# First feed-forward: unnormalized token halves, the inverse root applied to the gate and up products, context transposes within the projection

## What is computed

```python
def rms_norm(x, w):
    y = x * rsqrt(mean(x * x, -1) + EPS)
    return y * w
...
        mixed = concatenate([fox_out, hgrn_out], -1) @ w_out[l]
        h = h + mixed
        u = rms_norm(h, norm_ffn_w[l])
        h = h + (silu(u @ w_ffn_gate[l]) * (u @ w_ffn_up[l])) @ w_ffn_down[l]
```

## Time and profile before

| | us |
|---|---|
| median of 3 runs | 2755.51 |
| lowest, highest | 2754.37, 2759.36 |
| the profiled execution | 2757.04 |
| its span on the core | 2755.1 |

### The profile page before, as it was taken

How to read it: one execution, slowest core, us unless ns; L and a number is a source line. 1 busy time by engine, 2 the same in 40 slices (tenths; PEclk the granted TensorE clock), 3 DMA queues, 4 the chain that set the end, 5 groups by cost and what they waited for, 6 DMA issues and landing times.

```text
span 2755.1 us, 36972 instructions
## 1 busy us (share of the span) xinstructions
PE 2569.0 (93%) x14795; PEld 2198.5 (80%) x14795; DVE 1531.8 (56%) x2878; ACT 1096.7 (40%) x1928; POOL 321.7 (12%) x199
## 2 busy tenths in 40 slices
PE   7988889999997999998899999999899998999998
PEld 6787777878886877776788888888788787777877
DVE  3565547657747777677745443436455556533334
ACT  5544534222234655555521211114566556422222
POOL 2222100000012222121000000002223222000001
PEclk9999999999998999999899999999999999999999
DMA  4111033535521111111233333330323222222231
GB/s 118 47 39 51 19 107 122 176 124 181 169 84 47 39 39 39 31 39 39 69 100 123 104 110 113 103 123 24 73 52 73 52 53 60 73 96 86 96 108 47
DMA packets 247333, 223.86 MB, mean 81 GB/s; under 512 B 36916, under 2 KB 215898, under 8 KB 247162
## 3 DMA queue, kind: packets, MB, share of 16 engines
q1 hardware_dynamic: 247162, 221.49, 26.8%
HBM read 219.24 MB, written 2.22 MB: 80 GB/s over the span
## 4 chain that ended last, share of the span: by engine, by line
PE 77%; DVE 11%; ACT 7%; issue 4%; POOL 0%; DMA 0%; SPq 0%; DVEq 0%; POOLq 0%; ACTq 0%
PE ps L363 24%; PE ps L365 22%; PE ps L364 22%; DVE FR L527 2%; ACT FR L522 1%; PE ps L2815 1%; ACT whi L388 1%; PE ps L652 1%; PE ps L1071 1%; PE ps L2401 1%; ACT FA L2494 1%; PE ps L2826 1%; DVE hT L2574 1%; DVE FA L2614 1%; DVE raw L1444 1%
## 5 line engine op out<-in xcount | busy, mean ns | idle before, releaser
L363 PE MATMUL ps<-Uh,whi 128*128 128x512 f32 (+2 forms) x2544 | 904.2, 355 | 25.2 <-ACT FA L2513 5.9
L364 PE MATMUL ps<-Ul,whi 128*128 128x512 f32 (+2 forms) x2544 | 888.3, 349 | 0.0
L365 PE MATMUL ps<-Uh,wlo 128*128 128x512 f32 (+2 forms) x2544 | 887.8, 349 | 0.0
L363 PEld LDWEIGHTS ps<-Uh,whi 128*128 128x128 f32 x2544 | 491.2, 193 | 97.1 <-issue 20.0
L365 PEld LDWEIGHTS ps<-Uh,wlo 128*128 128x128 f32 x2544 | 489.7, 193 | 60.4
L364 PEld LDWEIGHTS ps<-Ul,whi 128*128 128x128 f32 x2544 | 491.2, 193 | 57.7
L388 ACT ACTIVATE whi<-raw 128x1024 fp32r<-128x1024 f32 (+2 forms) x205 | 296.4, 1446 | 555.0 <-PE ps L365 554.8
L399 DVE TENSOR_TENSOR wlo<-raw,whi 128x2048 fp32r<-128x2048 f32 (+2 forms) x121 | 248.3, 2053 | 299.3 <-ACT whi L388 299.1
L363 PE MATMUL ps<-FR,whi 128*128 128x512 f32 (+1 forms) x864 | 305.6, 354 | 24.9 <-DVE FR L527 20.1
L364 PE MATMUL ps<-FR,whi 128*128 128x512 f32 (+1 forms) x864 | 302.2, 350 | 0.0
L365 PE MATMUL ps<-FR,wlo 128*128 128x512 f32 (+1 forms) x864 | 301.8, 349 | 0.0
(11 more groups left out here) (334 smaller groups left out, 3289.0 us busy)
## 6 DMA issues: line engine op xcount, KB each, us to landing
FA<-in_ada_w_dram SPq DMA_DIRECT2D x192, 256.0 KB, 2.8
raw<-in_ffn_w_gate_up_dram SPq DMA_DIRECT2D x44, 1024.0 KB, 5.1
raw<-in_ffn_w_down_dram SPq DMA_DIRECT2D x24, 768.0 KB, 4.3
raw<-in_w_in_dram SPq DMA_DIRECT2D x29, 512.0 KB, 3.9
raw<-in_da_wqkv_dram SPq DMA_DIRECT2D x24, 512.0 KB, 3.7
raw<-in_na_wqkv_dram SPq DMA_DIRECT2D x24, 512.0 KB, 3.8
raw<-in_w_ffn_gate_dram SPq DMA_DIRECT2D x11, 1024.0 KB, 5.3
raw<-in_w_ffn_up_dram SPq DMA_DIRECT2D x11, 1024.0 KB, 5.4
```

Of the source, the lines that this page charges most:

```text
L363: e.matmul(out, ah, bh, start=start, stop=False)
L364: e.matmul(out, ah, bl, start=False, stop=False)
L365: return e.matmul(out, al, bh, start=False, stop=stop)
```

## The change

The high half of block n is made by ACT straight from `hT` with the weight column as scale, and the low half by DVE, both right behind the residual add of the block (`mixed_scalar`, `mixed_vector`). They lack the inverse root. The root is made as before, now into `st_acc`, while PE runs the first gate chunk: the ones matmul stands behind the first gate tile and uses bank 3. The first gate chunk goes tile by tile rather than through both tiles at once. In the feed-forward DVE multiplies each gate product by the root (`v_mul`, out of PSUM into `sil`), ACT takes silu there in place, and DVE multiplies by the root once more (`u_mul`), which stands for the root of the up product. `f_mul` then works as before. All sixteen transposes of the context stand behind block 5 of the projection, two blocks to a bank, and ACT's eight copies ahead of its work on block 6.

```diff
@@ norm_tensor, root_scalar: the bank is given as b; the root goes to st_acc
-        r = K.st_rs[:, t0:t1]
+        r = K.st_acc[:, t0:t1]
...
@@ norm_scalar and norm_vector are gone
@@ def mixed_tensor(K, e, w):
-    context_tensor(K, e, w, range(0, 4))
-    norm_tensor(K, e, w, "f0", (SX,))
-    context_tensor(K, e, w, range(4, 8))
+        if n2 == 2:
+            context_tensor(K, e, w)
@@ def mixed_scalar(K, e, w):
+        if n == 6:
+            for c in range(KC):
+                context_scalar(K, e, w, c)
         w.wait_ge(*K.at("o_add", n))
+        e.activation(K.Uh[:, n, 0:512], K.hT[:, n, 0:512], ACT.Identity, bias=K.zero[:, :], scale=K.cp(col("norm_ffn_w", n))).then_inc(
+            *K.ev("norm_hi", "f0", n, 0))
         square_scalar(K, e, w, "f0", n, 0, *SX)
-    root_scalar(K, e, w, "f0", (SX,))
-    for c in range(KC):
-        w.wait_ge(*K.at("norm_scaled", "f0", c, 0))
-        e.activation(K.Uh[:, c, 0:512], K.st_tmp[:, c % 2, 0:512], ACT.Identity, bias=K.zero[:, :]).then_inc(*K.ev("norm_hi", "f0", c, 0))
-        context_scalar(K, e, w, (0, 7, 1, 2, 3, 4, 5, 6)[c])
-        if c == 3:
-            split_hi(K, e, w)
+    split_hi(K, e, w)
+    root_scalar(K, e, w, "f0", (SX,), 3)
@@ def mixed_vector(K, e, w):
         e.tensor_tensor(hv, K.bank(n), hv, ALU.add).then_inc(*K.ev("o_add", n))
+        w.wait_ge(*K.at("norm_hi", "f0", n, 0))
+        halve_vector(K, e, hv, K.Uh[:, n, 0:512], K.Ul[:, n, 0:512], ("norm_lo", "f0", n, 0), K.cp(col("norm_ffn_w", n)))
         square_vector(K, e, w, "f0", n, 0, *SX)
-    norm_vector(K, e, w, "f0", (SX,), (SX,), lambda c, i: K.cp(col("norm_ffn_w", c)), lambda c, i: K.zero[:, :])
@@ def ffn_tensor(K, e, w, f):
-                o = K.hold(w, b, ("f_silu", st, m + n))[:, 0:t1 - t0]
+                o = K.hold(w, b, ("v_mul" if st == "f0" else "f_silu", st, m + n))[:, 0:t1 - t0]
...
-                project_first(K, e, w, st, len(f.segs), wh, wl, first)
+                for n, (j, i, t0, t1) in enumerate(f.tiles):
+                    t = project_piece(K, e, w, st, 0, first[n][0], wh, wl, t0, t1, j * P)
+                    t.then_inc(*K.ev("f_gate", st, n))
+                    if n == 0:
+                        norm_tensor(K, e, w, "f0", (SX,), 3)
@@ def ffn_scalar(K, e, w, f):
+            if st == "f0":
+                for n in (m, m + 1) if x == 0 else ():
+                    w.wait_ge(*K.at("v_mul", st, n))
+                    e.activation(K.sil[:, n % 2, :], K.sil[:, n % 2, :], ACT.Silu).then_inc(*K.ev("f_silu", st, n))
...
@@ def ffn_vector(K, e, w, f):
+            if x == 0 and st == "f0":
+                w.wait_ge(*K.at("norm_root", st, 0))
+                for n in (m, m + 1):
+                    w.wait_ge(*K.at("f_gate", st, n))
+                    w.wait_ge(*K.was("f_mul", st, n - 2))
+                    e.tensor_tensor(K.sil[:, n % 2, :], K.bank(K.xbank[st, n]), K.st_acc[:, 0:512], ALU.mult).then_inc(
+                        *K.ev("v_mul", st, n))
             if x == 0:
                 split_lo(K, e, w, "wlo_dve")
+            if x == 0 and st == "f0":
+                for n in (m, m + 1):
+                    w.wait_ge(*K.at("f_silu", st, n))
+                    e.tensor_tensor(K.sil[:, n % 2, :], K.sil[:, n % 2, :], K.st_acc[:, 0:512], ALU.mult).then_inc(
+                        *K.ev("u_mul", st, n))
```

More of the change, by code:

```diff
@@ L428, in square_vector, with norm_tensor, root_scalar @@
     e.tensor_tensor(acc, acc, K.st_sq[:, k, 0:t1 - t0], ALU.add).then_inc(*K.ev("square_sum", st, c, i))
-def norm_tensor(K, e, w, st, segs):
+def norm_tensor(K, e, w, st, segs, b):
     for i, (t0, t1) in enumerate(segs):
-        o = K.hold(w, i, ("norm_ln", st, i))[:, 0:t1 - t0]
+        o = K.hold(w, b + i, ("norm_ln", st, i))[:, 0:t1 - t0]
         w.wait_ge(*K.at("square_sum", st, KC - 1, i))
         e.matmul(o, K.ones[:, :], K.st_acc[:, t0:t1], start=True, stop=True).then_inc(*K.ev("norm_sum", st, i))
-def root_scalar(K, e, w, st, segs):
+def root_scalar(K, e, w, st, segs, b):
@@ L439, in root_scalar @@
     for i, (t0, t1) in enumerate(segs):
-        r = K.st_rs[:, t0:t1]
+        r = K.st_acc[:, t0:t1]
         w.wait_ge(*K.at("norm_sum", st, i))
-        e.activation(r, K.bank(i)[:, 0:t1 - t0], ACT.Ln, bias=K.eps[:, :], scale=1.0 / D).then_inc(*K.ev("norm_ln", st, i))
+        e.activation(r, K.bank(b + i)[:, 0:t1 - t0], ACT.Ln, bias=K.eps[:, :], scale=1.0 / D).then_inc(*K.ev("norm_ln", st, i))
         w.wait_ge(*K.at("norm_ln", st, i))
         e.activation(r, r, ACT.Exp, scale=-0.5).then_inc(*K.ev("norm_root", st, i))
-def norm_scalar(K, e, w, st, pieces, bcol):
-    for c in range(KC):
[L449 to L452, removed]
@@ L455, in norm_vector @@
[L455 to L470, removed]
@@ L1591, in mixed_sync, with context_tensor @@
         fetch_chunk(K, e, w)
-def context_bank(c):
-    return (c + 1) % 8
-def context_tensor(K, e, w, blocks):
+def context_tensor(K, e, w):
     w.wait_ge(*K.at("x0", "c"))
     w.wait_ge(*K.at("x1", "c"))
-    for c in blocks:
-        o = K.hold(w, context_bank(c), ("c_copied", c))
+    for c in range(KC):
+        o = K.hold(w, c // 2, ("c_copied", c + 1)) if c % 2 == 0 else o
         for t in range(2):
-            i = e.transpose(o[:, t * P:(t + 1) * P], K.ct[:, t, c * P:(c + 1) * P], K.ident[:, :])
+            a = c % 2 * 256 + t * P
+            i = e.transpose(o[:, a:a + P], K.ct[:, t, c * P:(c + 1) * P], K.ident[:, :])
         i.then_inc(*K.ev("c_turned", c))
 def context_scalar(K, e, w, c):
-    w.wait_ge(*K.at("c_turned", c))
-    e.activation(K.hT[:, c, 512:768], K.bank(context_bank(c))[:, 0:256], ACT.Copy).then_inc(*K.ev("c_copied", c))
+    w.wait_ge(*K.at("c_turned", c | 1))
+    e.activation(K.hT[:, c, 512:768], K.bank(c // 2)[:, c % 2 * 256:c % 2 * 256 + 256], ACT.Copy).then_inc(*K.ev("c_copied", c))
 def context_squares(K, e, w):
@@ L1751, in ffn_scalar @@
             j, i, t0, t1 = f.tiles[x]
-            w.wait_ge(*K.at("f_gate", st, m))
-            w.wait_ge(*K.was("f_lo", st, m - 2))
-            e.activation(K.sil[:, m % 2, 0:t1 - t0], K.bank(K.xbank[st, m])[:, 0:t1 - t0], ACT.Silu).then_inc(*K.ev("f_silu", st, m))
+            if st == "f0":
+                for n in (m, m + 1) if x == 0 else ():
+                    w.wait_ge(*K.at("v_mul", st, n))
+                    e.activation(K.sil[:, n % 2, :], K.sil[:, n % 2, :], ACT.Silu).then_inc(*K.ev("f_silu", st, n))
+            else:
+                w.wait_ge(*K.at("f_gate", st, m))
+                w.wait_ge(*K.was("f_lo", st, m - 2))
+                e.activation(K.sil[:, m % 2, 0:t1 - t0], K.bank(K.xbank[st, m])[:, 0:t1 - t0], ACT.Silu).then_inc(*K.ev("f_silu", st, m))
             if x == 0:
@@ L1789, in ffn_vector @@
             w.wait_ge(*K.at("f_up", st, m))
-            w.wait_ge(*K.at("f_silu", st, m))
+            w.wait_ge(*K.at("u_mul" if st == "f0" else "f_silu", st, m))
             e.tensor_tensor(mt, K.bank(4 + m % 2)[:, 0:t1 - t0], K.sil[:, m % 2, 0:t1 - t0], ALU.mult).then_inc(*K.ev("f_mul", st, m))
```

1 line of the change is left out of this document (removed).

## The result

| | before | after |
|---|---|---|
| median of the first five runs | 2755.21 | 2742.30 |
| lowest, highest | 2752.35, 2759.36 | 2737.84, 2747.04 |
| the profiled execution, its span | 2757.04, 2755.1 | 2742.30, 2740.5 |
| ratio, 95% interval | | 0.9957, 0.9946 to 0.9968 |

Two later comparisons of the same pair gave 0.9970 (0.9958 to 0.9982) and 0.9964 (0.9951 to 0.9977). The three together are near 0.9964, about 10 us. So two things need an explanation: some 2.5 us beyond the forecast in all three together, and some 3 us that only the first comparison had. The times alone do not show the first: a saving of 7.5 us is a ratio of 0.9973, which lies outside the first interval but inside both later ones.

What follows compares the result with a forecast made beforehand. PE, busy 93% of the span, was taken to bound the kernel. Closing its gap (-7.6 us) plus DVE lag (+0.1) gave -7.5: 2749.5 us for the profiled execution, 2748.0 as median; 8-in-10 range 2745 to 2753.5.

Steps and rivals of the forecast that it cites:

- What bounds the kernel, and the gap: PE, busy 93%, bounds the kernel; closing its gap between output projection and feed-forward turns 65.03 us into 57.4.
- A: PE from the first projection matmul to the first one-column matmuls (L652), 110.95 us before; 7.6 us less forecast.
- The split of the 7.6 into idle time and clock: Behind the projection: 4.5 us idle time, 2.6 us slow clock (13 matmuls at 0.427 rather than 0.227), the rest shorter transposes.
- The halves and the root beside the projection: Halves made in PE's shadow during the projection; block 7's ready with 2.5 us margin, so PE starts the gate at once.
- The products: Root products in the feed-forward: 30 us more DVE work, f_mul 1.4 us late, margin 1.5 us, cost 0.1 (0 to 5.6).
- T: End of a gate chunk in the feed-forward; DVE steps are timed from it, the first f_mul at T+6.95.
- Partial lag at slice ends: Rival: DVE's lag makes PE wait one us at each of four feed-forward slice ends, 2752; chance 0.18.
- Clock at the transposes: Rival: sixteen transposes in the projection cost one slow stretch, 2.6 us, 2750.6; chance 0.11 together with late halves.
- DVE as the bound: Rival: in the feed-forward each of 11 pairs pushes PE by 1.4 us, +7.8, 2763.3; chance 0.05.
- The sum: Whole kernel: -7.6 + 0.1 = -7.5 us, from 2757.04 to 2749.5 profiled, or 2748.0 as median.
- with a slow stretch elsewhere that falls half as long (1.3): More-gain case, whole kernel: no lag, short transposes and a low run reach 2746.6, with this 2745.3; chance 0.06.
- B and C: PE stretches after A, to the first tail matmul, then to the second block's second query group; no saving forecast there.

## Why the prediction missed, step by step

**What bounds the kernel, and the gap.** Right. The gap behind the projection closed, and with it the slow stretch behind it. Forecast for A: 7.6 less; measured 7.95 and 7.98. The transposes cost 1.66 us rather than 2.0 and the ones matmul about 0.9 rather than 0.97.

**The split of the 7.6 into idle time and clock.** Right as a sum, wrong as a price: "2.6 us slow clock" stood for something that can be had by itself, and the run with a filled gap gave 1.6. The slow clock and the late halves covered each other.

**The halves and the root beside the projection.** Right: block 7's low half starts at 424.48 with the gate already running, and no PE row waits.

**The products.** Right in course and size. With T = 434.5, f_mul was forecast at T+6.95 and T+11.7, the next pair at T+23.5, the low half of the third up weights at the end of T+42.1; measured 6.7, 11.4, 23.0 and 41.3. The margin was forecast as 1.5 us and is 3.9 (475.77 to 479.63): the low half came 0.8 us earlier than forecast, and PE wants it 1.5 us later, because the sums of L652 stand ahead of the third up chunk; I had counted their 1.7 us for f_mul and not here. The cost, forecast at 0.1 between 0 and 5.6, is 0 by the run without products.

**The rivals.** Partial lag at slice ends: not there, three waits of 5.2 us in all as before. Clock at the transposes: not there; the Trainium skill ("TensorE: Matmul & The Clock Gate", Part 4: PE-mode transpose) says that transposes do not count as PE work for the clock as matmuls do. Sixteen in a row, 1.7 us between matmuls, stayed at 1.00 in two kernels; that does not refute the page for longer rows of them, which no run here has. DVE as the bound: shown possible only with the products doubled.

**The sum, where the prediction failed.** "It would come to 2749.5" took the rest of the program over unchanged from one profile. This is the step that failed. It put at nothing a term that is not nothing: every later wait of PE meets the clock at another moment once all before it is 8 us shorter. That term was in the text only as "with a slow stretch elsewhere that falls half as long (1.3)", in a case of 0.06. It is real and repeats in each profile of the two kernels for the next 470 us of program: +0.7 in B and -2.1 to -2.7 in C, together 1.4 to 2.0 us. The run with 35 extra matmuls and the one with the transposes alone show that it belongs to the moment at which the waits come, not to the edit.

On top of it the rest of a profile varies by 4 us between launches of one kernel (1790.6 and 1794.9 for before, 1789.8 to 1793.5 for after). The first pair of profiles differs by 14.6 us in its spans: 7.95 in A, 2.0 in B and C, 5.1 in the rest, less 0.5 ahead of the projection. So of the 5.4 us by which the first comparison beat the forecast about 0.4 are A, about 2 are B and C, and the other 3 were luck of the draw, which the two later comparisons did not have. The miss is not all luck, though: the three medians of the changed kernel, 2742.3, 2744.3 and 2743.1, all lie below 2745. The range was too narrow on this side: with an unknown of 2 to 3 us for the clock of later waits it would have begun at about 2742.

**Open.** Why B and C repeat from launch to launch while the rest is drawn anew, and what decides between eleven and thirteen slow matmuls at the start of A, is not shown by these runs. All stretches were read from one profile of each run with an edit.

## What to carry to other kernels

Let a normalization's factor go through a linear product, and apply it where the engine that has time meets the result: the matmuls can then start on unnormalized halves. When PE's idle time is cut early in a program, count the change, and then allow some microseconds either way for the slow stretches behind all later waits; a filler of the saved length helps to tell the two apart, with more than one profile, since a launch has a draw of its own. And look in a chain of accumulating matmuls for a wait placed ahead of the first step that only the last one needs: moving it was worth twice the change studied here.

## What was not expected of the hardware

The slow stretches (granted clock 0.50) behind one and the same wait differ between launches of one kernel from about 956 us on, which moves that part by up to 4.3 us, but repeat to 0.1 us in the stretches A to C of the changed kernel over three launches. One stretch inside A has 11 slow matmuls in eleven profiles and 13 in three, worth 0.5 us. A slow stretch can cost less than its matmuls suggest: 13 matmuls at 0.427 us instead of 0.227 are 2.6 us, and without it PE was only 1.6 us faster. DVE's products of 128x512 with one operand in PSUM and with both in SBUF took the same: 0.69 us alone (`v_mul` at 434.61 and, in before, L428), and 1.28 for two in a row (`v_mul` at 457.54, `u_mul` at 440.02).
